# RWKV and mixture-of-experts kernel: modulation sums of the later blocks on VectorE, the gate projection in single steps, direct first gathers

## What is computed

```
c_act = silu(c)
mod   = c_act @ w_ada + b_ada                      # 3072 values, block 1
h     = rms_norm(x, g) * (1 + scale) + shift
proj  = h @ w_in
r, k, v, g = shifted columns of proj               # 512 each, 4 head pairs of 128
y_r   = rwkv7(r, k, v, ...)                        # 8 heads of 64
x     = x + gate * (concat(y_r * silu(g_r), y_a * silu(g_a)) @ w_out)
...
mod_2 = silu(c_2) @ ada_w_2 + ada_b_2              # 6144 values: block 2 and the experts
weights, experts = top 2 of 32 for each row
out   = final_norm(x + sum of weight * expert(h_3))
```

## Time and profile before

| | |
|---|---|
| median of three runs | 1395.49 us |
| the profiled execution's own time | 1391.97 us |
| its span | 1389.9 us, mean TensorE clock 0.98 |
| TensorE matmul busy | 1292.5 us, 93% |
| TensorE weight loads | 640.0 us, 46% |
| VectorE | 559.7 us, 40% |
| ScalarE | 351.2 us, 25% |
| GpSimd | 160.5 us, 12% |
| read from memory | 299.5 MB, 225 GB/s over the span |

### The profile page before, as it was taken

How to read it: one execution, slowest core, us unless ns; L and a number is a source line. 1 busy time by engine, 2 the same in 40 slices (tenths; PEclk the granted TensorE clock), 3 DMA queues, 4 the chain that set the end, 5 groups by cost and what they waited for, 6 DMA issues and landing times.

```text
span 1389.9 us, 21101 instructions
## 1 busy us (share of the span) xinstructions
PE 1292.5 (93%) x7560; PEld 640.0 (46%) x7561; DVE 559.7 (40%) x1034; ACT 351.2 (25%) x759; POOL 160.5 (12%) x278
## 2 busy tenths in 40 slices
PE   5999999999999998999999998999999987897777
PEld 1445656568954444554445545433333333332222
DVE  1366363655214333349786635312212212121115
ACT  1223231422135442221467510101111101110102
POOL 4011010101120000000000001411121111111110
PEclk9999999999999999999999999999999999999999
DMA  9250704323163110014112384789999999999995
GB/s 365 84 212 11 279 26 167 138 79 149 35 187 147 46 46 1 0 49 167 52 57 76 122 348 182 276 350 396 411 412 419 399 406 421 403 402 416 409 391 209
DMA packets 40420, 303.93 MB, mean 219 GB/s; under 512 B 7964, under 2 KB 8116, under 8 KB 22800
## 3 DMA queue, kind: packets, MB, share of 16 engines
q1 hardware_dynamic: 31808, 285.12, 52.3%
q0 software_dynamic: 8528, 17.67, 4.1%
HBM read 299.49 MB, written 13.75 MB: 225 GB/s over the span
## 4 chain that ended last, share of the span: by engine, by line
PE 74%; DMA 14%; DVE 6%; issue 2%; ACT 2%; POOL 1%; DVEq 0%; SPq 0%; ACTq 0%; POOLq 0%
PE bank L858 21%; PE bank L2874 12%; DMA arena<-in_w_down 11%; PE bank L790 8%; PE bank L2892 7%; PE bank L904 4%; PE bank L969 2%; PE bank L847 2%; PE bank L2862 2%; DMA arena<-in_ada_w 1%; PE bank L1186 1%; PE bank L1130 1%; PE bank L1107 1%; PE bank L893 1%; PE bank L2883 1%
## 5 line engine op out<-in xcount | busy, mean ns | idle before, releaser
L858 PE MATMUL bank<-hT,arena 128*128 128x512 f32 x720 | 320.0, 599 | 0.0
L2874 PE MATMUL bank<-arena,hT 128*64 128x512 f32 x1024 | 231.9, 603 | 18.0 <-DMA arena<-in_w_gu 17.6
L858 PEld LDWEIGHTS bank<-hT,arena 128*128 128x128 f32 x720 | 135.0, 191 | 162.6 <-issue 159.2
L2874 PEld LDWEIGHTS bank<-arena,hT 128*64 128x64 f32 x1024 | 72.9, 138 | 156.3 <-issue 138.1
L2892 PE MATMUL bank<-arena,yT 128*64 128x512 f32 x512 | 123.8, 628 | 15.7 <-DMA arena<-in_w_down 13.9
L790 PE MATMUL bank<-arena,yT 128*128 128x512 f32 x256 | 114.5, 601 | 2.4 <-DVE yT L1685 2.3
L3062 DVE TENSOR_SCALAR hT<-hT 128x256 f32<-128x256 f32 x32 | 9.4, 295 | 248.4 <-ACT hT L3000 248.4
L3000 ACT ACTIVATE hT<-bank 128x256 f32<-128x256 f32 x32 | 12.3, 384 | 264.0 <-PE bank L2874 264.0
L790 PEld LDWEIGHTS bank<-arena,yT 128*128 128x128 f32 x256 | 48.1, 192 | 60.0 <-issue 56.2
L2892 PEld LDWEIGHTS bank<-arena,yT 128*64 128x64 f32 x512 | 36.1, 143 | 78.7 <-issue 61.2
L904 PEld LDWEIGHTS bank<-arena 64*64 64x64 f32 x1856 | 59.3, 135 | 23.8 <-issue 14.4
(11 more groups left out here) (489 smaller groups left out, 1609.1 us busy)
## 6 DMA issues: line engine op xcount, KB each, us to landing
arena<-in_w_gu SPq DMA_DIRECT2D x63, 2048.0 KB, 26.8
arena<-in_w_down SPq DMA_DIRECT2D x32, 2048.0 KB, 30.5
arena<-in_w_in SPq DMA_DIRECT2D x53, 512.0 KB, 4.6
arena<-in_ada_w SPq DMA_DIRECT2D x24, 1024.0 KB, 5.1
arena<-in_w_ada SPq DMA_DIRECT2D x8, 1024.0 KB, 9.1
arena<-in_w_out SPq DMA_DIRECT2D x8, 1024.0 KB, 9.0
arena<-in_w_ada SPq DMA_DIRECT2D x8, 512.0 KB, 4.7
arena<-expert_rows SPq DMA_DIRECT2D x4, 1024.0 KB, 8.4
```

Of the source, the lines that this page charges most:

```text
L858: last = T.matmul(bank[0:rows, :], w[:, k, 0:rows], hT[:, k, :], start=k == 0, stop=k == KD - 1)
L2874: last = T.matmul(banks[1 + ub][MT * h:MT * h + MT, :], tile.xT[:, k, :], wgu[u][:, k // 4, k % 4, :, 256 * h:256 * h + 256], start=k == 0 ...
```

## The change

Groups 0 and 1 stay on TensorE; group 1's k-steps now stand together, after pair 0's value projection. For groups 2 to 4 VectorE multiplies each slot by its scalar per partition and adds it to a running sum of 128 x 2048 (`mod_part`; the first of a group is a plain multiply), and TensorE sums that over the partitions by four matmuls with ones (`mod_rows`); VectorE adds the bias (`mod_made`). Of the 24 parts four stand in the tail of each of pairs 0 to 2 and twelve in the last pair. From part 14 on every second slot is in a third buffer. The gate projection of a pair is made in the pair itself, in eight single k-steps at the places of the modulation's (in the last pair in four blocks of two), and the next pair's no longer at level 4; `operands` moves behind the adds of level 4, and the gate's exponential and clamp into the next pair. GpSimd stores group 4's row and loads the columns after the attention bias. The router makes the row weights later; the first seven gathers take their indices straight from `slots`; the first refill of expert weights is sent in quarters.

```diff
@@ start-up, TensorE
             lora(0)
+            key_norm(0)
             pe_proj(("proj", 0, 2))
-            key_norm(0)
             eng.wait_ge(s_first_in, 1)
-            for k in range(3):
-                pe_ada(1, k)
-            pe_proj(("proj", 0, 3))
-            for k in range(3, KD):
+            for k in range(KD):
                 pe_ada(1, k)
             bonus(0)
+            def mod_rows(g):
+                eng.wait_ge(s_ada_used, KD * (g + 1))
+                bank = fill(("mod", g))
+                for j in range(4):
+                    last = T.matmul(bank[32 * j:32 * j + 32, :], ones[:, 0:32], mod_sum[:, 512 * j:512 * j + 512],
+                                    start=True, stop=True)
+                full(last)
@@ pair loop, TensorE
-                if not q:
-                    eng.wait_ge(s_mod, 5)
-                ada_step()
+                if p == 2:
+                    mod_rows(2)
                 va_rows(1)
...
                     blocks(("W", p, l), Lfc[l % 2], Dc, (0, 1))
-                    if l <= 4 and q:
+                    if l <= 3 and q:
                         pe_proj(("proj", q, PROJ_ORDER[l - 1]))
-                    elif q and l == LEVELS - 2:
-                        ada_step()
+                    elif q:
+                        gate_steps(1)
                     else:
+                        if l == 3:
+                            mod_rows(3)
+                        if l <= 4:
+                            gate_steps(2)
                         va_rows(2 if l <= 4 else 1)
...
-                ada_step()
+                if q:
+                    gate_steps(1)
...
             mean(PAIRS - 1)
+            mod_rows(4)
             pe_proj(("aproj", 0, 0))
@@ VectorE
+        def mod_part(i):
+            g, k = 2 + i // KD, i % KD
+            slot, loaded, at = ada_slot(g, k)
+            c = cact[:, KD + k:KD + k + 1]
+            V.wait_ge(loaded, at)
+            if k:
+                dve.done(V.scalar_tensor_tensor(mod_sum, slot, c, mod_sum, MUL, ADD))
+            else:
+                if g > 2:
+                    V.wait_ge(filled, fill_at[("mod", g - 1)] + 1)
+                dve.done(V.tensor_scalar(mod_sum, slot, c, None, MUL))
+            V.sem_inc(s_ada_used, 1)
...
                 if q:
                     decay_clamp(q)
+                else:
+                    mod_part(12)
+                    mod_part(13)
                 level_add(p, 2)
+                if not q:
+                    mod_part(14)
+                    mod_part(15)
...
+                if not q:
+                    mod_made(3)
                 level_add(p, 3)
                 if q:
                     proj_shift(q, 2)
-                    operands(q)
+                else:
+                    mod_part(16)
+                    mod_part(17)
                 level_add(p, 4)
                 if q:
-                    proj_shift(q, 3)
+                    operands(q)
+                else:
+                    proj_shift(p, 3)
+                    mod_part(18)
+                    mod_part(19)
...
+                parts = iter(range(4 * p, 4 * p + 4) if q else range(20, 24))
+                mod_part(next(parts))
                 for c in range(TT - 1):
+                    mod_part(next(parts))
                     bank = take(V, ("S", p, c))
@@ SyncE
+                    if n == 2 * KD + LATE:
+                        sp.wait_ge(filled, fill_at[("gram", PAIRS - 1, 1, 4)] + 1)
+                        sp.wait_ge(s_ops, 3 * PAIRS - 2)
...
-        ada_after = {("proj", 0, 3): KD + 1, ("proj", 1, 3): KD, ("proj", 2, 3): KD, ("proj", 3, 3): KD - 1}
+        ada_after = {("proj", 0, 2): KD, ("proj", 0, 3): 2, ("proj", 2, 2): 4, ("proj", 3, 2): 4, ("va", 1): 4,
+                     ("va", 2): 2, ("va", 3): 4, ("aproj", 0, 0): 4}
@@ experts, SyncE and GpSimd
+            def first_next_gate_up(u, e):
+                p, n = slot_before(e)
+                eng.wait_ge(more_.gate_up, n + 1)
+                stand_alone(eng)
+                for half, (steps_done, at) in enumerate(((first.half_done, 1), (first.gate_up, 2))):
+                    eng.wait_ge(s_slots, SLOTS + 1 + half)
+                    load_quarter(u, e, half, 0, w_gu[u][half])
+                    eng.wait_ge(steps_done, p + at)
+                    stand_alone(eng)
+                    load_quarter(u, e, half, 1, w_gu[u][half])
...
+            def gather_known(tile, e):
+                eng.indirect_dma_start(tile.xg, None, xn_dram, bass.IndirectOffsetOnAxis(ap=slots[:, e:e + 1], axis=0),
+                                       bounds_check=SEQ - 1, oob_is_err=False).then_inc(tile.gathered, 16)
```

More of the change, by code:

```diff
@@ L161, in plan, with plan_on @@
             fills.append((name, by))
+        def plan_on(name, by, bank):
+            held[name] = bank
+            plan(name, by)
+            free_banks[0].remove(bank)
         def plan_proj(p, j):
@@ L416, in build_program @@
         w2sb = phase.take(D_RWKV)
-        t_ld, t_cum, t_exc, t_yn, t_inv, t_a, t_rn, t_kk, t_k2, t_b = (phase.take(SEQ) for _ in range(10))
+        t_ld, t_cum, t_exc, t_yn, t_inv = (phase.take(SEQ) for _ in range(5))
+        LATE_AT = phase.at
+        t_a, t_rn, t_kk, t_k2, t_b = (phase.take(SEQ) for _ in range(5))
         t_bonus = [phase.take(SEQ) for _ in range(2)]
@@ L971, in va_rows, with gate_steps @@
                             full(last)
[L973 to L976, removed]
+                def gate_steps(count):
+                    name = ("proj", p, 3)
+                    if not p and not gate_k[0]:
+                        eng.wait_ge(s_mod, 2)
+                    w = chunk_ready(name)
+                    for _ in range(count):
+                        k = gate_k[0]
+                        gate_k[0] += 1
+                        bank = fill(name) if k == KD - 1 else begin(name)
+                        last = T.matmul(bank[:, :], w[:, k, :], hT[:, k, :], start=k == 0, stop=k == KD - 1)
+                        if k == KD - 1:
+                            full(last)
                 eng.wait_ge(s_ops, 3 * p + 1)
@@ L1217, in va_out @@
             def va_out(n):
+                if not n:
+                    eng.wait_ge(s_ada_used, 2 * KD + LATE)
                 bank = take(S, ("va", n))
@@ L1306, in act_block1 @@
                         key_square(q)
-                    if l <= 4 and q:
+                    if l <= 3 and q:
                         proj_raw(q, l - 1)
+                    if l == 4 and not q:
+                        proj_raw(p, 3)
                     if l in (2, 4) and not q:
@@ L1399, in act_block1 @@
                     act_sigmoid(("agate", p + 1), (aegs[:, (p + 1) % 2, :], None))
+        items = [(0, n) for n in range(3)]
+        for p in range(PAIRS - 1):
+            items += [(p + 1, n) for n in range(3)] + [(p, 3)]
+        items.append((PAIRS - 1, 3))
+        ITEM = {name: n + 1 for n, name in enumerate(items)}
         squares = [("key", 0)]
@@ L2863, in turn_rows, with gate_up @@
                 last.then_inc(tile.xf, 1)
-            def gate_up(tile, steps, u, n, ub, it=None, last_quarter=False):
+            def gate_up(tile, steps, u, n, ub, it=None, last_quarter=False, quarters=False):
                 eng.wait_ge(steps.xT, n + 2)
@@ L2871, in gate_up @@
                     if it is not None and k % 4 == 0:
-                        eng.wait_ge(w_gu[u][k // 4], (it + 1) * 16)
+                        eng.wait_ge(w_gu[u][k // 4], (it + 1) * 16 + (16 if not u and (not isinstance(it, int) or it) else 0))
                     for h in range(2):
@@ L2875, in gate_up @@
                                         wgu[u][:, k // 4, k % 4, :, 256 * h:256 * h + 256], start=k == 0, stop=k == KD - 1)
+                    if quarters and k in (1, 5):
+                        last.then_inc(s_slots, 1)
                     if k == KD // 2 - 1:
@@ L2910, in first_experts @@
                 turn_rows(tiles[1], first, 1, 0, 7, True)
-                gate_up(tiles[0], first, 0, 0, 0, 0)
+                gate_up(tiles[0], first, 0, 0, 0, 0, quarters=True)
                 turn_last_hot()
```

173 lines of the change are left out of this document (113 added, 60 removed).

## The result

In six runs each, the changed kernel has a median of 1402.84 us (1398.94 to 1406.80), the kernel before 1394.99 (1394.29 to 1395.78). The ratio is 1.0068, with a 95% interval of 1.0054 to 1.0083. Forecast was 1394.3 with a range from 1388.5 to 1400; the kernel was expected unchanged and became slower. One execution in the experiments, the ninth of twelve of the first, took 4447.44 us and is left out.

A forecast was written before the change was run, and what follows sets the result against it. TensorE was taken to bound the pair loop, weight loads the experts. Start-up -6.5, pairs 0 to 2 -15.1, last pair +20.85 and the rest -0.4 sum to -1.15, put onto the median: 1394.3 us, range 1388.5 to 1400.

The forecast's parts named there:

- Start-up: Before pair 0: gate projection leaves, key norm's matmul moves ahead of the value projection; transposes begin at 79.2, -6.5 us.
- Pairs 0 to 2: First three pairs: modulation k-steps and next gate projection out, single gate k-steps and some waits in; -15.1 us in all.
- lone gate steps: Eight single gate k-steps in each of pairs 0 to 2: 1.05 us each, 8.4 us per pair.
- the lower bound: Lone gate steps at 0.88 us each, as inside the stream, instead of 1.05.
- Last pair: Last pair of the loop: added gate steps, row sums, waits on VectorE and a clock drop; +20.85 us.
- I take the same +1.7 here: Last pair, after a TensorE wait of over 5 us: lower clock for 16 matmuls, 5.35 instead of 3.65 us.
- Clock (slower): Rival: lower clock after each TensorE wait, twice as long after the long one; +5.3, 1400.8 us; chance 0.2.
- The row that spoke against it: Pair 0, evidence against the clock rival: a 1.9 us wait there is followed by no clock drop.
- Direct gathers: nothing: Experts' start: direct gathers save GpSimd a copy and a 1.2 us wait each, but the first row turn waits for VectorE; nothing.
- Quarter loads: nothing: Experts' first refill: SyncE restarts 2.2 us sooner but then waits for TensorE to free a slot; nothing, as a bound -2.2.
- the shift did not stay within 0.5 us: Sign: from the first expert on, the shift stays within 0.5 us of what block 1 gave.
- It doesn't relieve TensorE: Rival, tails of pairs 0 to 2: third sum late by slow loads, 1.5 us each; +3.2, 1398.7 us; chance 0.08.

The follow-up runs named there:

- the first: Changed kernel with the expert gathers as before (GpSimd copies each index column first): 1399.05 us, ratio 1.0035.
- the repaired kernel: Changed kernel with gathers and refill as before, group 3's row sums a level later, group 2's in the modulation's bank, dummy matmuls in waits: 1385.57 us, ratio 0.9946.
- The filled waits: Changed kernel with 34 dummy matmuls in front of TensorE's new waits: 1407.24 us, ratio 1.0096; with 16 dummies 1397.13 us, ratio 1.0025.
- the last kernel above: Repaired kernel with the last pair's sums spread out, only the first expert gather direct and the first refill in quarters: 1382.38 us, ratio 0.9912.
- the one with short sums: Changed kernel with the last pair's twelve sums 64 columns wide instead of 2048, without running total: 1400.13 us, not comparable as a whole.

## Why the prediction was wrong

It named the mechanisms and the places of the waits, and gave the clock a single 1.7 us, in the last pair. In stretches of 1 us the profile after shows 30.7 us of the loop at the lower level (the expectation above counts 27.3), the kernel before none; by the terms below that is some 11 us of time.

- **Start-up.** -6.36 against -6.5, in part by luck: of thirteen profiled executions with this start-up 79.33 is the earliest beginning of pair 0, the others have 80.06 to 81.89, a gain of 3.8 to 5.6 us.
- **Pairs 0 to 2.** The lone gate steps take the forecast 1.05 among the products of the levels, but in the tail three of four take 0.86 from their start to the next group's, as at 300.69: the lower bound, and eight in some 7.8 instead of 8.4. The waits at level 4 (0.57) and level 6 (0.56) are those forecast (0.65, 0.55). Held at full clock, with pair 2's bank free (the repaired kernel), the pairs take 72.2, 74.4 and 74.1 us, 17.8 less than before, even better than the -15.1. The changed kernel kept 11.8 of it. Two things took the rest. A bank: the row sums of group 2 take one from the rotation, so that the next projection gets one which still holds a gram mask (1.86 us); the prediction gave these matmuls 1.0 us of work and overlooked what their bank stands in front of. And the clock, for which the sum had nothing here: 3.4 us at the lower level in each of the three, about 1.7 us of time.
- **Last pair.** Waits of 2.3, 5.3 and 3.2 us were forecast as 1.5, 5.5 and 2.75, so the sizes hold to 1 us. The forecast 9.4 us of work and the 10.8 of waits leave 5.7 of the +25.9 to the clock, where the step "I take the same +1.7 here" stands. That is the term that failed, 1.7 for 5.7, together with the nothing that stands for the 5.1 of the first three pairs: the clock fell for 14 us, not for one group, and for 7 us more at the wait before level 6. The size was wrong and not the mechanism; filling the waits took the loss away.
- **The rival had it.** "Clock (slower)", in which every long wait brings the lower clock, gave 1400.8 and got 0.2. The row that spoke against it, a wait of 1.9 us in pair 0 without a drop, was read rightly: it stands so in all three profiled executions of kernels with that loop. But it doesn't carry over. In six kernels whose pair 1 has a wait of 1.88 us the clock of that stretch shows 0.98 three times and 1.00 three times; the wait of 1.86 in pair 2 brought it in all five that have it, that of 2.93 in pair 0 in five of six. The first row is of the kernel before, the next two of the changed one, the last two of the one with both expert parts undone:

```profile
93.14 1.15 PE L904 MATMUL bank<-arena 64*64 64x64 f32 x32 [1.94 <-POOLq L680]
...
160.40 1.15 PE L946 MATMUL bank<-arena 64*64 64x64 f32 x32 [1.88 <-POOLq L719]
161.47 8.82 PE L900 MATMUL bank<-hT,arena 128*128 128x512 f32 x16
...
163.68 1.15 PE L946 MATMUL bank<-arena 64*64 64x64 f32 x32 [1.88 <-POOLq L719]
164.76 7.13 PE L900 MATMUL bank<-hT,arena 128*128 128x512 f32 x16
```

What decides between these cases no run shows. Beside these rows the Trainium skill's page "TensorE: Matmul & The Clock Gate", section "A second HAM failure mode: psum-queue depth-cycling", tells of a kernel in which short idle gaps between groups of matmuls come often enough to make the clock go back and forth. The filled waits agree that idle time brings it; here single waits of about 2 us did.
- **The experts.** "Direct gathers: nothing" was wrong. The copy that they save also kept GpSimd's gathers apart (870.25, 872.36 and 874.38 before); closer, VectorE's step is held for 1.6 us, and the turn comes 1.6 to 1.9 us later. The prediction looked at who waits for the gather, not at who shares something with the engine that sends it. The Trainium skill's page "SBUF — State Buffer", section "Who interferes with whom", says that GpSimd and some VectorE operations exclude each other on a pair of ports for a whole instruction. The small row beside agrees with that: the next VectorE step from SBUF to SBUF takes 0.54 us under GpSimd's memset and 0.25 without. The held step reads PSUM and not SBUF. By the same section a VectorE instruction with at most one input in SBUF, outside the modes that use both ports, doesn't contend; so the page doesn't explain it, and its cause stays open. "Quarter loads: nothing" held.
- **From the router to the end** the shift did not stay within 0.5 us. Five profiled executions with all gathers direct take 526.4 to 529.0 us there, nine others 519.9 to 525.2, and the last kernel above 526.6 (the one with short sums, which routes other rows, left aside). The clock there is 0.94 to 0.95 in the first, 0.95 to 0.97 in the others. Whether the direct gathers bring that, beyond their 1.6 to 1.9 us, or chance does, isn't settled; taken alone on the kernel before they cost 0.1%. So of the 7.7 us by which the profiled span missed behind the loop, most has no shown cause.
- **"It doesn't relieve TensorE"**, the rival with late third sums, shows as waits of VectorE for loads in the tails of pairs 0 to 2, 0.83, 1.72, 1.05 and 0.96 us, without a wait of TensorE behind them.

## What to carry to other kernels

Where TensorE is busy all the time, a new wait costs its length and can cost, on top, a stretch at half clock, which here took 1.7 us of time or more. Price a wait of 2 us or more twice, and don't take a wait without a drop, even in three traces, as proof for another place. Before a consumer is moved, look for the level at which its input is ready anyway: one position cost 7 us of the last pair here. Where a wait can't be moved, matmuls that compute nothing, sized below the wait, keep the clock (5.5 us of loop for 11 of them). And a bank taken from a rotation delays whoever gets the next one.

## What was not expected of the hardware

A run of three indirect DMAs on GpSimd, 0.3 us apart, held a VectorE operation that reads PSUM until the third was sent (1.6 us), in all six kernels that had them; with 1 us between them it fell due in a gap and wasn't held. Waits of 1.9 and 2.3 us were enough for the lower clock to be granted, though not each time, and a profile's spread of 8 us between runs of one program goes with it: the six runs of the changed kernel had clocks of 0.977 (1398.94 us) down to 0.962 and 0.965 (1406.74 and 1406.80), with one of 0.964 at 1402.17.
